# Expert loop of a mixture-of-experts block: the down product moved one block later, weights loaded in halves, the down weights loaded from GpSimd's queue

## The reference

```python
# h: (2048, 1024) float32; every token goes to 2 of 32 experts; rows are sorted
# by expert and padded to blocks of 128 rows of one expert each
def expert_block(args):
    xb, e = args
    hid = jax.nn.silu(xb @ w_gate[e]) * (xb @ w_up[e])   # 128x1024 @ 1024x512, twice
    return hid @ w_down[e]                               # 128x512 @ 512x1024
out = lax.map(expert_block, (rows.reshape(n_blocks, 128, -1), block_e)).reshape(n_rows, -1)
# then each token sums its two rows, weighted, is added to x, and a last RMSNorm follows
```

## Time and profile before

| what | value |
|---|---|
| median of 3 runs | 2601.83 us (2600.53 to 2602.84) |
| the profiled execution: its time, its span | 2598.93 us, 2597.2 us |
| mean granted clock of TensorE | 0.923 |
| first gate matmul of the expert loop | 1542.63 us |
| store of the last block issued | 2503.06 us |
| busy shares over the span: PE, DVE, ACT, POOL | 84%, 55%, 43%, 11% |
| bytes moved | 458.76 MB |

### The profile page before, as it was taken

The page is one execution under the profiler, slowest core; times in us unless marked ns, Lnnn a source line. Parts: engine busy times, 40 slices in busy tenths (PEclk is TensorE's granted clock), DMA queues, the critical chain, the costliest instruction groups (busy, mean ns, idle before and its releaser), DMA issues. The chain is left out here.

```text
span 2597.2 us, 29608 instructions
## 1 busy us (share of the span) xinstructions
PE 2193.0 (84%) x9806; PEld 1650.3 (64%) x9807; DVE 1421.5 (55%) x2441; ACT 1110.1 (43%) x1586; POOL 276.6 (11%) x348
## 2 busy tenths in 40 slices
PE   4999999948969687876999549999999999999950
PEld 3764444448447576765888437777777777777740
DVE  4831582045258576674544557566648847354548
ACT  6101111012317576665222126566647847355432
POOL 0002331024220110000000000000000000000022
PEclk6999999979869898998999759999999999999985
DMA  7023443172742514311433158477758958454649
GB/s 223 33 73 138 170 142 118 41 245 112 314 112 69 114 27 88 86 29 51 134 128 134 51 218 347 186 282 279 279 210 340 370 227 333 168 198 195 253 172 378
DMA packets 128019, 458.76 MB, mean 177 GB/s; under 512 B 25136, under 2 KB 41536, under 8 KB 113600
## 3 DMA queue, kind: packets, MB, share of 16 engines
q1 hardware_dynamic: 98352, 345.22, 38.0%
q0 software_dynamic: 18928, 69.49, 7.1%
q10 hardware_dynamic: 10656, 43.00, 4.0%
HBM read 342.06 MB, written 115.61 MB: 176 GB/s over the span
## 5 line engine op out<-in xcount | busy, mean ns | idle before, releaser
L1533 DVE TENSOR_TENSOR w_gate_lo<-w_gate_raw,w_gate_hi 128x2048 fp32r<-128x2048 f32 x64 | 146.3, 2286 | 179.0 <-ACT w_gate_hi L1488 179.0
L895 DVE CUSTOM_DVE_ANT_0 scores<-c_bank,alibi 128x512 f32<-128x512 f32 (+3 forms) x320 | 175.4, 607 | 109.0 <-PE c_bank L993 108.8
L488 PE MATMUL a_bank<-w_in_chunk,hT 128*128 128x512 f32 x512 | 221.9, 596 | 0.7 <-ACT hT L266 0.7
L488 PE MATMUL a_bank<-hT,w_in_chunk 128*128 128x512 f32 x512 | 220.6, 593 | 0.0
L300 ACT ACTIVATE proj_out<-a_bank 128x512 f32<-128x512 f32 x64 | 38.2, 597 | 398.7 <-PE a_bank L488 389.4
L488 PEld LDWEIGHTS a_bank<-w_in_chunk,hT 128*128 128x128 f32 x512 | 128.8, 252 | 92.7 <-issue 62.6
L1007 PE MATMUL c_bank<-v_head,map_T 128*128 128x128 f32 x1088 | 152.2, 289 | 41.7 <-ACT map_T L951 41.7
L1576 PE MATMUL m_bank<-w_gate_hi,rows_T_hi 128*128 128x512 f32 x392 | 154.9, 395 | 24.2 <-DVE rows_T_lo L1537 24.2
L1614 PE MATMUL m_bank<-w_down_hi,hidden_T_hi 128*128 128x512 f32 x392 | 160.4, 409 | 16.2 <-ACT hidden_T_hi L1510 16.2
L488 PEld LDWEIGHTS a_bank<-hT,w_in_chunk 128*128 128x128 f32 x512 | 97.0, 190 | 120.9 <-issue 120.8
L1007 PEld LDWEIGHTS c_bank<-v_head,map_T 128*128 128x128 f32 x1088 | 136.2, 198 | 57.4 <-ACT map_T L951 57.4
(11 more groups left out here) (375 smaller groups left out, 4427.0 us busy)
## 6 DMA issues: line engine op xcount, KB each, us to landing
w_gate_raw<-in_w_gate_dram SPq DMA_DIRECT2D x32, 2048.0 KB, 7.8
w_up_raw<-in_w_up_dram SPq DMA_DIRECT2D x32, 2048.0 KB, 10.7
w_down_raw<-in_w_down_dram SPq DMA_DIRECT2D x32, 2048.0 KB, 10.7
rows_d<-rows_out ACTq DMA_DIRECT2D x50, 512.0 KB, 10.3
rows_d<-zero_rows POOLq DMA_DIRECT2D x34, 512.0 KB, 18.6
x_tile<-in_x_dram SPq DMA_DIRECT2D x16, 512.0 KB, 3.8
w_in_chunk<-in_w_in_dram POOLq DMA_DIRECT2D x4, 2048.0 KB, 14.9
qT_d<-xn_tile SPq DMA_DIRECT2D x32, 256.0 KB, 3.1
```

The lines of the kernel that those rows point to most:

```text
L488: last = pe.matmul(bank[4 + n % PB][:], lhsT, rhs, start=kt == 0, stop=kt == KT - 1)
L895: dve.tensor_tensor_reduce(S[:, s, m, c * BANK:c * BANK + w], bank[n % 4][:, 0:w], bias[:, h % 2, x0:x0 + w], 1.0, -BIG, ALU.add, ALU.max, ...
L1533: dve.tensor_tensor(wlo[w][:, s], raw[w][:, s], whi[w][:, s], ALU.subtract).then_inc(lo_done[w], 1)
```

## The change

The down product of block b is done after the gate and up products of block b+1. The first block's gate and up products stand ahead of the loop, and the last block's down product behind it. The transposes of the hidden rows go between the gate and the up product of the next block. All three weights are loaded in halves of 1 MiB, each with its own semaphore and its own wait for one half of `lo_done`; SyncE loads gate and up, and GpSimd loads down, from its own queue. ScalarE copies both output halves. `preload_act_table(ACT.Silu)` stands ahead of ScalarE's loop, and the first rows are split ahead of the first weights. `meta` gets one entry more, the number of blocks less one, and the list of experts one more place. Each loop reads more registers from `meta` at its head.

```diff
+            def load(eng, w, e, i):
+                k = FT if w == 2 else KT
+                src = a[name_of[w]][0, bass.ds(e, 1)].rearrange("o (p k) n -> p (o k n)", k=k)
+                eng.dma_start(raw[w][:, halves[i]], src[:, halves[i]]).then_inc(w_in[w][i], 16)
             @block.sync
-                    for w, name in enumerate(("w_gate", "w_up", "w_down")):
-                        sp.wait_ge(hi_done[w], 2 * o + 2)
-                        sp.wait_ge(lo_done[w], 2 * o + 2)
-                        sp.dma_start(raw[w][:], a[name][0, bass.ds(e, 1)].rearrange("o (p k) n -> p (o k n)", k=k)).then_inc(w_in[w], 16)
+                    for w in range(2):
+                        for i in range(2):
+                            sp.wait_ge(lo_done[w], 2 * o + 1 + i)
+                            load(sp, w, e, i)
             @block.gpsimd
+                gather(0)
+                first, second = expert(pool, 0), expert(pool, 1)
+                for i in range(2):
+                    load(pool, 2, first, i)
...
+                with pool.Fori(2, n) as b:
+                    past, now = place(pool, b - 2), place(pool, b - 1)
+                    e = expert(pool, now + 1)
+                    pool.wait_ge(xT_psum, 2 * b + 2)
+                    gather(b + 1)
+                    with where_below(nc, pool, past, now):
+                        for i in range(2):
+                            pool.wait_ge(lo_done[2], 2 * now + 3 + i)
+                            load(pool, 2, e, i)
             @block.scalar
+                with act.Fori(0, later(act)) as j:
+                    before, now, order = place(act, j), place(act, j + 1), place(act, j + 2)
+                    hidden_hi(j + 1)
+                    act.wait_ge(g_done, j + 2)
+                    act.wait_ge(hid_done, j + 1)
                     act.activation(sil[:], G[:], ACT.Silu).then_inc(silu_done, 1)
...
             @block.tensor
+                with pe.Fori(0, later(pe)) as j:
+                    before, order = place(pe, j), place(pe, j + 1)
...
+                    product(G, 0, g_done)
+                    hidden_T(j)
+                    pe.wait_ge(hi_done[1], 2 * order + 4)
+                    pe.wait_ge(lo_done[1], 2 * order + 4)
+                    product(U, 1, u_done)
+                    pe.wait_ge(x_in, 16 * j + 48)
+                    rows_T(0)
+                    rows_T(1)
+                    down(j, before)
+                end = later(pe)
+                hidden_T(end)
+                down(end, place(pe, end))
```

More of the change, by code:

```diff
@@ L1431, in experts @@
         out = sb("rows_out", [P, D])
-        w_in = [sem(f"w_{n}_in") for n in ("gate", "up", "down")]
+        w_in = [[sem(f"w_{n}_in{i}") for i in range(2)] for n in ("gate", "up", "down")]
         hi_done = [sem(f"w_{n}_hi_done") for n in ("gate", "up", "down")]
@@ L1483, in _, with split_hi @@
+                n = blocks(pool)
+                end = place(pool, n - 2)
+                for i in range(2):
+                    pool.wait_ge(w_in[2][i], 16 * end + 32)
             @block.scalar
             def _(act):
[L1485 to L1488, removed]
+                def split_hi(w, order, i):
+                    act.wait_ge(w_in[w][i], 16 * order + 16)
+                    act.activation(whi[w][:, halves[i]], raw[w][:, halves[i]], ACT.Copy).then_inc(hi_done[w], 1)
@@ L1496, in _, with store @@
+                def store(b):
+                    act.wait_ge(d_used, 2 * b + 4)
+                    act.dma_start(d["rows"][bass.ds(b, 1)].rearrange("o p n -> p (o n)"), out[:]).then_inc(out_st, 16)
+                act.preload_act_table(ACT.Silu)
                 rows_hi(0, 1)
                 rows_hi(1, 2)
[L1498 to L1504, removed]
+                for w in range(3):
+                    split_hi(w, 0, 0)
+                    split_hi(w, 0, 1)
@@ L1522, in _ @@
-                    act.dma_start(d["rows"][bass.ds(b, 1)].rearrange("o p n -> p (o n)"), out[:]).then_inc(out_st, 16)
-                n = blocks(act)
-                act.wait_ge(out_st, 16 * n + 16)
+                        split_hi(1, order, 1)
+                    out_half(1, j)
+                    store(j)
+                    with where_below(nc, act, before, now):
+                        split_hi(2, now, 0)
+                        split_hi(2, now, 1)
+                end = later(act)
@@ L1525, in _ @@
+                hidden_hi(end + 1)
+                out_half(0, end)
+                out_half(1, end)
+                store(end)
+                act.wait_ge(out_st, 16 * end + 32)
                 act.activation(last_copy[:], ones[:, 0:1], ACT.Copy)
@@ L1528, in _, with split_lo @@
             def _(dve):
[L1529 to L1533, removed]
+                def split_lo(w, order, i):
+                    dve.wait_ge(hi_done[w], 2 * order + 3 + i)
+                    dve.tensor_tensor(wlo[w][:, halves[i]], raw[w][:, halves[i]], whi[w][:, halves[i]],
+                                      ALU.subtract).then_inc(lo_done[w], 1)
                 def rows_lo(h, want):
@@ new lines, in _ @@
+                for w in range(3):
+                    split_lo(w, 0, 0)
+                    split_lo(w, 0, 1)
+                first, second = place(dve, 0), place(dve, 1)
+                with where_below(nc, dve, first, second):
+                    split_lo(0, second, 0)
+                    split_lo(0, second, 1)
+                hidden(0)
+                rows_lo(0, 3)
+                rows_lo(1, 4)
+                with where_below(nc, dve, first, second):
+                    split_lo(1, second, 0)
+                    split_lo(1, second, 1)
@@ L1565, in _ @@
+                end = later(dve)
+                hidden_lo(end + 2)
             @block.tensor
```

170 lines of the change are left out of this document (97 added, 73 removed).

## The result

The changed kernel takes 2530.39 us (median of 4 runs, 2527.12 to 2537.76) against 2602.18 (2600.53 to 2602.84) before: a ratio of 0.973, 95% interval 0.9705 to 0.9753.

A forecast was written before the change was run, and what follows sets the result against it. TensorE was taken as the loop's bound, with two round trips to remove: 1549.9 + 893 + 6.2 + 1 + 4 = 2454 for TensorE's end against 2502, 48 us less, so 2554 us; range 2543 to 2581.

The forecast's parts named there:

- the two round trips: TensorE's waits for `hidden` and the copy `hidden_T_hi` in every block, 23.1 and 16.2 us per 400 us, would go.
- the price of a block, 18.6 us: In the loop, 72 matmuls at 0.233 us plus 12 transposes, 18.54 us, taken as 18.6; 48 blocks make 893 us.
- 4 us lost to the DMA engines in the run of seven: Seven gate loads in a row: loads take up to 1.2 us a block too long, less cover of about 3 us.
- The bare round trip at the end, 1 us: Ahead of the last down product, behind the loop: one uncovered wait of TensorE, about 1 us.
- The start: Ahead of the loop: the second block's gate product starts at 1549.9, 14.6 us earlier than at 1564.55.
- DMA bound: Rival, chance 0.16: runs of new experts cost the full 17 us and down loads come late; 2562 to 2582 us.
- the starved issue on GpSimd: Within the DMA rival: GpSimd's down loads wait for VectorE's low halves, up to 64 us of lateness, 10 us counted.
- Register reads: Rival, chance 0.09: a second read at the head of TensorE's loop costs up to 48 us; 2575 to 2602 us.
- ScalarE bound: Rival, chance 0.08: ScalarE has 1 us of room per block, uncounted reads and branches exceed it; 2607 us and up.
- More than I count: Rival, chance 0.09: no loss to DMA, transposes at 0.11 us, a start some us better; 2535 to 2545 us.

The follow-up runs named there:

- one_stop: Changed kernel with the hidden transposes back between the two row transposes, so TensorE waits for the copy `hidden_T_hi` again: 2572.72 us, 0.9917 of the kernel before.
- old_start: Changed kernel with the first rows split behind the first weights, as before the change: 2545.06 us, 0.9784 of the kernel before.
- sp_lag: Changed kernel with all weights on SyncE's queue, gate and up of the next expert ahead of the present one's down: 2529.15 us, 0.9745 of the kernel before.
- act_plus2: Changed kernel with two more ScalarE copies of 128x2048 behind each new expert's down split: 2551.42 us, 0.9835 of the kernel before.
- act_plus4: Changed kernel with four more ScalarE copies of 128x2048 behind each new expert's down split: 2667.71 us, 1.0269 of the kernel before.
- sp_down: Changed kernel with the down weights back on SyncE's queue, in the order gate, up, down: 2613.43 us, 1.0064 of the kernel before.

## Why the prediction was wrong, point by point

- **The bound and the two round trips**: right. Both waits are gone, and one_stop brings one back with its time. But 2 of the 39 us in the earlier trace rows were the late gate load and no round trip.
- **The step that failed is the price of a block, 18.6 us**, made of "12 transposes, four in 0.58 us, 1.74 us" and rounded up. It measured 18.16: 48 x 0.44 = 21 us. The 0.58 was read from the first four transposes behind a stop, 1907.78 to 1908.36, and in it was the price of starting again. Transposes in a row cost 0.10 to 0.11, 1.2 for the twelve; the two changes to matmuls behind them cost 0.17, where the prediction had 0.06. That the stops cost 1.30 us in an ordinary block and not the 0.82 that the earlier trace rows show is the same mistake seen from the other side.
- **4 us lost to the DMA engines in the run of seven**: none. The second error was to turn "at full share that is 395 GB/s" into a loss: at shares of 1.00 to 1.01 they moved 397 to 417 GB/s, while a block of 7.34 MB in 18.16 us asks for 404.
- **The bare round trip at the end, 1 us**: wrong. The last down product waits for the split of its weights, which can't begin before the product ahead of it ends. With the slow matmuls behind it, the end took 16.8 us for the forecast 7.2, 9.6 more.
- **The start**: right within 2 us (1548.0 for 1549.9), and old_start shows that 12 of the 16.5 us won are the rows split first.
- Together: -21.3 - 4 + 9.6 - 1.9, and 1.3 for the slow clock in the second gate product, is 16.3 us below the forecast end of 2454; measured 2437.7. The other 7 us of the miss in the median are where the profiled execution stands: 7.4 above its median, which the forecast took to be 2.9 below, less the 2.9 us of the phases ahead. Errors of both signs met here: without the end, the forecast of TensorE's end would have been off by 26 us, not 16.
- **Rivals.** DMA bound: refuted, since no block was longer at shares of 1.00 to 1.01, and with it the starved issue on GpSimd. Its 64 down loads took 527 to 612 ns to issue and no split waited for them, though VectorE was reading SBUF; so these subtractions of two SBUF tensors didn't starve the loads. The Trainium skill (SBUF — State Buffer, Who interferes with whom) has them contend with GpSimd's reads of SBUF, but it also says that a `tensor_tensor` did not stall DMAs in its own probe; the trace agrees with that. What it says of issuing engines (DMA: Bandwidth & Descriptors, Issuing engines are not separate DMA queues) is borne out by sp_lag: one queue is as fast as two. Register reads: refuted, with 3.1 us of cover. ScalarE bound: refuted as it stands, but its mechanism is real, and by an estimate from act_plus2 and act_plus4 the kernel would be slower than before with some 5.7 us more work per new expert (3.4 + 72 / 31); the rival had 4.7. "More than I count" was the nearest, with its transposes at 0.11 and no loss to DMA; the result is still 5 us below its 2535 to 2545.
- **The range** left this case out but for a third. Its two large widenings went to the slower side.

## What to carry to other kernels

Read the price of a short operation from a stretch in which nothing has just stopped: a row behind a wait holds the restart too, and a removed stop is worth its idle time and 0.1 to 0.3 us more. Where one queue waits for several buffers in turn, its order must be the order in which they come free; when a step is moved a block later, its load has to move in the queue with it, or the loads behind it can come late, as nine blocks in sp_down showed. And lay out the last pass of a pipelined loop by itself: what the loop hides behind the next block has nothing to hide behind there.

## What was not expected of the hardware

- A register read at the head of TensorE's loop costs about 0.65 us once nothing hides it, and about 3.1 us of them were free.
- The DMA engines moved 397 to 417 GB/s at shares of 1.00 to 1.01, over four 18 us windows, while TensorE never waited.
- A stop of TensorE cost 0.23 to 0.25 us more than its row shows, at two different places.
- Behind 4.0 us without work TensorE's next product ran at a mean granted clock of 0.77, behind 6.8 us at 0.60, and behind 2.6 us at 1.00 in sp_lag and 0.76 in old_start. Work that is started earlier and then waits can lose what it won.
